# Hybrid S5 and short-convolution encoder block on eight cores: half-array products side by side, rotation products without their sum, and a finer TensorE order in the S5 stage

## The reference, cut to what matters

```python
h = rms_norm(h_stream, g_mix_pre)
u_s, x_c, b_c, c_c, gl_s, gl_c = split(h @ w_in)
# branch S: per group of 16 channels 64 complex states, forward and backward
ar, ai = exp(lr*dt)*cos(li*dt), exp(lr*dt)*sin(li*dt)
s[t] = (ar + i*ai) * s[t-1] + z * (B @ u_s[t])        # associative scan
y_s  = D*u_s + sum over both directions of  Re(C @ s)
y_s  = gelu(y_s); y_s = y_s * sigmoid(y_s @ w_glu + b_glu); y_s = y_s @ w_s_up
# branch C
y_c  = (b_c * dwconv3(c_c * x_c)) @ w_c_up
merged = sigmoid(gl_s + gb_s)*y_s + sigmoid(gl_c + gb_c)*y_c
h_stream = h_stream + rms_norm(merged @ w_o)
gate, up = split(rms_norm(h_stream) @ w_ffn_in)
h_stream = h_stream + rms_norm((silu(gate)*up) @ w_ffn_out)
```

## Time and profile before

| | |
|---|---|
| Median of 3 runs | 1840.55 us (1840.54 to 1956.79) |
| The profiled execution: time of the run | 1844.34 us |
| its span on core 1, the slowest | 1843.3 us (all cores 1825.6 to 1843.3) |
| PE busy in the span | 1766.2 us (96%), 9744 matmuls |
| DVE busy | 701.7 us (38%) |
| ACT busy | 496.3 us (27%) |
| granted clock, mean of core 1 | 0.991 |

### The profile page before, as it was taken

How to read it: one execution, slowest core, us unless ns; L and a number is a source line. 1 busy time by engine, 2 the same in 40 slices (tenths; PEclk the granted TensorE clock), 3 DMA queues, 4 the chain that set the end, 5 groups by cost and what they waited for, 6 DMA issues and landing times.

```text
span 1843.3 us, 25331 instructions; the slowest of 8 cores (1825.6 to 1843.3 us)
## 1 busy us (share of the span) xinstructions
PE 1766.2 (96%) x9744; PEld 848.0 (46%) x9744; DVE 701.7 (38%) x820; ACT 496.3 (27%) x948; POOL 118.0 (6%) x226
## 2 busy tenths in 40 slices
PE   3999999999999979889999999999999999999998
PEld 2664555544444434334444444444444444444443
DVE  4475999887786524425620110110110010101023
ACT  4554665545555420014420000000000000101010
POOL 0000000000001011100000000000000000000000
PEclk9999999999999989999999999999999999999999
DMA  9754444466667878974554446464555441443457
GB/s 236 192 152 103 79 82 83 78 114 133 123 118 160 182 143 190 220 167 138 182 121 80 69 80 112 69 112 80 100 98 94 69 79 33 77 81 66 91 126 243
DMA packets 87510, 219.06 MB, mean 119 GB/s; under 512 B 34080, under 2 KB 34592, under 8 KB 80832
## 3 DMA queue, kind: packets, MB, share of 16 engines
q0 software_dynamic: 31744, 121.71, 39.3%
q1 hardware_dynamic: 52480, 90.58, 16.4%
q10 hardware_dynamic: 3168, 5.15, 0.8%
HBM read 303.32 MB, written 35.72 MB: 184 GB/s over the span
## 4 chain that ended last, share of the span: by engine, by line
PE 82%; DMA 12%; DVE 2%; issue 2%; ACT 1%; SPq 1%; POOL 0%; ACTq 0%; DVEq 0%; POOLq 0%
PE ps L219 82%; DMA yr<-yc_d 5%; DMA wus<-w_in 2%; DMA wr<-w_in 2%; DMA xin<-xseq 1%; DMA gs_d<-tc 1%; DMA gT<-g_d 1%; PE ps L225 1%; SPq L213 1%; DMA gs_d<-ys 1%; DMA xr<-xseq 0%; DVE mgd L244 0%; DVE Pt L255 0%; POOL wus L213 0%; ACT Xt L235 0%
## 5 line engine op out<-in xcount | busy, mean ns | idle before, releaser
L219 PE MATMUL ps<-hN,wf 128*128 128x512 bf16 x2816 | 608.1, 379 | 0.0
L219 PEld LDWEIGHTS ps<-hN,wf 128*128 128x128 bf16 x2816 | 275.4, 98 | 331.8
L219 PE MATMUL ps<-hT,wr 128*128 128x512 bf16 (+1 forms) x1888 | 368.8, 351 | 5.3 <-DMA wr<-w_in 4.0
L219 PE MATMUL ps<-wfo,agr 128*128 128x512 bf16 x1408 | 304.1, 379 | 0.0
L241 DVE TENSOR_TENSOR agr<-ps,sgt 128x512 bf16<-128x512 f32 x88 | 60.9, 692 | 535.8 <-PE ps L219 535.8
L219 PEld LDWEIGHTS ps<-hT,wr 128*128 128x128 bf16 x1888 | 178.8, 97 | 175.9 <-issue 15.1
L219 PEld LDWEIGHTS ps<-wfo,agr 128*128 128x128 bf16 x1408 | 137.8, 98 | 166.1
L235 ACT ACTIVATE sgt<-ps 128x512 f32<-128x512 f32 x88 | 52.6, 598 | 535.0 <-PE ps L219 535.0
L219 PE MATMUL ps<-wo,mgd 128*128 128x512 bf16 x512 | 114.6, 386 | 5.6 <-DVE mgd L244 4.8
L241 DVE TENSOR_TENSOR facc<-ps,gp2a 128x512 f32<-128x512 f32 x24 | 16.6, 692 | 212.2 <-ACT sqj L235 151.4
L235 ACT ACTIVATE sqj<-ps 128x512 bf16<-128x512 f32 x32 | 19.1, 598 | 265.3 <-PE ps L219 265.3
(11 more groups left out here) (136 smaller groups left out, 1361.4 us busy)
## 6 DMA issues: line engine op xcount, KB each, us to landing
wf<-w_ffn_in POOLq DMA_DIRECT2D x88, 512.0 KB, 5.7
wr<-w_in POOLq DMA_DIRECT2D x51, 512.0 KB, 6.5
wfo<-w_ffn_out POOLq DMA_DIRECT2D x16, 1408.0 KB, 9.7
...
```

Source lines behind the costliest of these rows:

```text
L219: return lambda e: e.matmul(o, lhsT=l, rhs=r, start=st, stop=sp)
```

## The change

- PE: rotated-back states are no longer summed. The cosine products go to `Gt` and the sine products to a new bf16 tile `Gq`, both straight from DVE, and `out_stage` multiplies both with `M1`: 32 half products for each `(b, d)` where 16 stood (256 more in all); DVE loses one 128x1024 addition for each.
- The 16 full products `Mst` x `Ub` now stand together ahead of the half products; in `scan_stage` the four products are ordered so that neighbours go to different halves of the output.
- `prep1` makes each complex product with three real products: 10 operations of 1024 and two of 256 where 12 of 1024 stood, from two more tables (`ASUM`, `WSUM`).
- `trig`'s range reduction goes from a DVE multiply with rounding into int32 to an ACT Identity with a large bias.
- `pB` and `go` have one buffer each, no longer two. `gT` is eight tiles with keys of their own, b=0 to 4 lying on `ptmp` and `Wt` only.
- For the order: half products count half the cost, the least cost of a matmul is 0.02 and no longer 0.06 us, and D's matmul groups of 16 go in pieces of 8, between which S may come.

```diff
+    PIECE = 8
@@ mms
-        self.add("pe", fns, sum(max(0.06, it[5] / 2400.0 + 0.0025) for it in items), reads, writes, lag=lag)
+        n = self.PIECE if self.stream == "D" else len(items)
+        for i in range(0, len(items), n):
+            part = items[i:i + n]
+            self.add("pe", [one(*it[:5]) for it in part], sum(max(0.02, it[5] / 2400.0 + 0.0025) for it in part), reads, writes, lag=lag)
@@ tables
+    S.tt(ASUM, ARE[:, 0:512], AIM[:, 0:512], ALU.add, 512, [kr, ki, ("wtab", 0), ("wtab", 1)], [("tbK", 2)])
+    S.tt(WSUM, WR, WI, ALU.add, 512, [("wtab", 0), ("wtab", 1), ("tbK", 2)], [("tbK", 3)])
...
+    S.ts(sv(s_phi), sv(s_phi), 1.0 / TWO_PI, None, ALU.mult, None, 64, [sk(s_phi)], [sk(s_phi)])
@@ prep1
-        S.tt(v4(ta), cc(BR), aa(WR), ALU.mult, 1024, [pk, w0], [ka])
-        S.tt(v4(tb), cc(BI), aa(WI), ALU.mult, 1024, [pk, w1], [kb])
+        S.tt(bsum[:], re2, im2, ALU.add, 256, [pk], ["bsum"])
+        S.tt(im2, im2, re2, ALU.subtract, 256, [pk], [pk])
+        S.tt(v4(ta), cc(BR), aa(WSUM), ALU.mult, 1024, [pk, kw_s], [ka])
+        S.tt(v4(tb), cs(0), aa(WI), ALU.mult, 1024, ["bsum", w1], [kb])
         S.tt(ww(0), ta, tb, ALU.subtract, 1024, [ka, kb], [("Wt", 0)])
-        S.tt(v4(ta), cc(BI), aa(WR), ALU.mult, 1024, [pk, w0], [ka])
-        S.tt(v4(tb), cc(BR), aa(WI), ALU.mult, 1024, [pk, w1], [kb])
+        S.tt(v4(tb), cc(BI), aa(WR), ALU.mult, 1024, [pk, w0], [kb])
         S.tt(ww(1), ta, tb, ALU.add, 1024, [ka, kb], [("Wt", 1)])
@@ trig
-        S.ts(tB[:, 0:W], tA[:, 0:W], 1.0 / TWO_PI, None, ALU.mult, None, W, TK, ["trB"])
-        S.stt(tA[:, 0:W], tB[:, 0:W], -TWO_PI, tA[:, 0:W], ALU.mult, ALU.add, W, TK + ["trB"], TK)
+        S.act(tB[:, 0:W], tA[:, 0:W], AF.Identity, W, TK + [("small", 60)], ["trB"], bias=magic)
+        S.stt(tA[:, 0:W], tB[:, 0:W], MAGIC, tA[:, 0:W], ALU.subtract, ALU.subtract, W, TK + ["trB"], TK)
@@ scan_stage
-            for hh in range(2):
-                for ri in range(2):
+            for ri in range(2):
+                for hh in range(2):
...
-        S.tt(o3(1024), zs, cs, ALU.mult, 1024, PK + ["CO%d" % d], ["Qt", "Qt_hi"])
-        S.tt(o3(0), zs, ss, ALU.mult, 1024, PK + SK, ["Qt"])
-        S.tt(Gt[:, d, :, :, :].rearrange("p r a k -> p r (a k)"), Qt[:, 1024:2048].rearrange("p (r k) -> p r k", r=2), swap(Qt, 512), ALU.add, 1024,
-             ["Qt", "Qt_hi"], [("Gt", d)])
+        S.tt(Gt[:, d, :, :, :], zs, cs, ALU.mult, 1024, PK + ["CO%d" % d], [("Gt", d)])
+        S.tt(Gq[:, d, :, :, :], zs, ss, ALU.mult, 1024, PK + SK, [("Gq", d)])
@@ out_stage
+            if d == 0:
+                for gq in range(4):
+                    for dd in range(2):
+                        for hh in range(2):
+                            items.append((o(hh, gq), Mst[p][:, dd, hh, gq, :], UB[p][:, 4 * hh + gq, 2:130], gq == 0 and dd == 0, False, 128))
             for gq in range(4):
...
+                for gt, ri, gi in ((Gt, 0, 0), (Gq, 0, 1), (Gt, 1, 1), (Gq, 1, 0)):
...
-        go, gk = GO[b % 2], "go%d" % (b % 2)
+        gk = "go0"
@@ M stream
-    gT = S.tile("gT", [128, 8, 8, 128], BF16, 160384)
+    gT = [S.tile("gT%d" % b, [128, 8, 128], BF16, 162432 + 2048 * b) for b in range(8)]
...
-            S.dma(q, gT[16 * g8:16 * g8 + 16, b, :, :], src, 32768, "gT%d%s" % (b, q), reads=[("g_d", b)], writes=[("gT", b, g8)])
+            S.dma(q, gT[b][16 * g8:16 * g8 + 16, :, :], src, 32768, "gT%d%s" % (b, q), reads=[("g_d", b)], writes=[("gT%d" % b, g8)])
```

More of the change, by code:

```diff
@@ L25 @@
 SIN_S = 1.0 - 1e-5
+MAGIC = 1.5 * 2.0 ** 23
 NCORES = 8
@@ L219, in one @@
             return lambda e: e.matmul(o, lhsT=l, rhs=r, start=st, stop=sp)
-        fns = [one(*it[:5]) for it in items]
-        self.add("pe", fns, sum(max(0.06, it[5] / 2400.0 + 0.0025) for it in items), reads, writes, lag=lag)
+        n = self.PIECE if self.stream == "D" else len(items)
+        for i in range(0, len(items), n):
+            part = items[i:i + n]
+            self.add("pe", [one(*it[:5]) for it in part], sum(max(0.02, it[5] / 2400.0 + 0.0025) for it in part), reads, writes, lag=lag)
     def transposes(self, items, reads, writes, early=100000):
@@ L470, in _program @@
     S.memset(halfpi, math.pi / 2, [], [("small", 63)])
+    magic = small[:, 60:61]
+    S.memset(magic, MAGIC, [], [("small", 60)])
     LRE, LIM, LDT = lam[:, 0:64], lam[:, 64:128], lam[:, 128:192]
@@ L619, in _program @@
     Gt = S.tile("Gt", [128, 2, 2, 4, 128], BF16, 131712)
+    Gq = S.tile("Gq", [128, 2, 2, 4, 128], BF16, 141952)
     yt = S.tile("yt", [128, 8, 128], F32, 135808)
-    GO = [S.tile("go%d" % i, [128, 8, 128], BF16, 139904 + 2048 * i) for i in range(2)]
+    go = S.tile("go0", [128, 8, 128], BF16, 139904)
     def load_u(b):
@@ L659, in scan_stage @@
             items = []
-            for hh in range(2):
-                uv = UB[p][:, 4 * hh + gq, :]
-                rhs = uv[:, 0:NP] if d == 0 else mk(uv, [[-1, NP]], off=NCH - 1)
-                for ri in range(2):
-                    items.append((bs[ri][0][64 * hh:64 * hh + 64, 0:NP], Vst[p][:, d, hh, gq, 64 * ri:64 * ri + 64], rhs, True, True, NP))
+            for ri in range(2):
+                for hh in range(2):
+                    uv = UB[p][:, 4 * hh + gq, :]
+                    rhs = uv[:, 0:NP] if d == 0 else mk(uv, [[-1, NP]], off=NCH - 1)
+                    items.append((bs[ri][0][64 * hh:64 * hh + 64, 0:NP], Vst[p][:, d, hh, gq, 64 * ri:64 * ri + 64], rhs, True, True, NP // 2))
             S.mms(items, ukeys(b) + [("Vst%d" % p, d, 0), ("Vst%d" % p, d, 1)], [bs[0][1], bs[1][1]])
@@ L840, in _program @@
             q = "sp" if b < 7 else ("sp", "act", "pool")[g8 % 3]
-            S.dma(q, gT[16 * g8:16 * g8 + 16, b, :, :], src, 32768, "gT%d%s" % (b, q), reads=[("g_d", b)], writes=[("gT", b, g8)])
-    GK = [("gT", b, g8) for b in range(8) for g8 in range(8)]
+            S.dma(q, gT[b][16 * g8:16 * g8 + 16, :, :], src, 32768, "gT%d%s" % (b, q), reads=[("g_d", b)], writes=[("gT%d" % b, g8)])
+    GK = [("gT%d" % b, g8) for b in range(8) for g8 in range(8)]
     g3 = S.tile("g3", [128, 8, NTOK], BF16, 180416)
@@ L849, in _program @@
     GS = [S.tile("gs%d" % i, [128, NTOK], F32, 164032 + 4096 * i) for i in range(2)]
-    gT2 = gT[:].rearrange("p b i n -> p b (i n)")
+    gT2 = [flat(t[:]) for t in gT]
     WK = [("wgl", kq) for kq in range(4)]
     def glu(m, blk, pb, pk, ks):
-        S.mms([(pb[:], wgl[:, k, 128 * m:128 * m + 128], gT2[:, k, 512 * blk:512 * blk + 512], k == 0, k == 7, 512) for k in ks],
-              WK + [("gT", k, g8) for k in ks for g8 in range(8)], [pk])
+        S.mms([(pb[:], wgl[:, k, 128 * m:128 * m + 128], gT2[k][:, 512 * blk:512 * blk + 512], k == 0, k == 7, 512) for k in ks],
+              WK + [("gT%d" % k, g8) for k in ks for g8 in range(8)], [pk])
     first = {}
@@ L879, in _program @@
         if m in EARLY:
-            ei = EARLY.index(m) % 2
+            ei = sorted(EARLY).index(m) % 2
             gs, gk = GS[ei], ("gs%d" % ei,)
```

53 lines of the change are left out of this document (26 added, 27 removed).

## The result

The changed kernel takes 1850.2 us in the median of its runs, the kernel before 1840.9 on the same chip. The ratio is 1.0051 with a 95% interval of 1.0028 to 1.0075: some 9 us slower, where 12.4 us less were forecast. It is less than 2% and so within what was called no change, but the sign is wrong and the time lies outside the range of 1818 to 1846.

What follows compares the result with a forecast made beforehand. PE was taken to bound the kernel while S and D are mixed, DMA the merge stage. The terms summed to -12.4 us: 1844.3 to 1831.9, less 3.8 for the runs' median, 1828 us; range 1818 to 1846.

Steps and rivals of the forecast that it cites:

- More half products: PE in S5: 256 more half products at 28.8 ns each, +7.4 us, bounds 0.0 and 14 us.
- no pairs: Rival: new `Gt` and `Gq` products on PE don't run in pairs, 13.9 us instead of 7.4, 1835 us; chance 0.07.
- Changes of shape: PE's whole order: 193 changes between full and half products instead of 205, at 0.106 us each, -1.3 us.
- `Vst` products: S5's `Vst` products on PE: already run in pairs, so reordering them gains 0.
- the other bound: `Vst` products on PE: if they did not already run in pairs, one pass less would gain 5.2 us.
- DVE and ACT: S5's elementwise work: some 35 us less on DVE, an Identity more per direction on ACT, covered by PE's work: 0.
- One buffer for `pB` and `go`: S5 blocks: the load and store take 7.8 us within a block of some 50 us, so covered: 0.
- `gT` loads earlier: D's last 40 us: fewer `gT` loads on SP free the `gs_d` stores; PE's `Xt` wait -3.2 us, slow clock -1.2 us.
- The boundary: D's end to GLU's other 86 matmuls: 9.1 us instead of 21.0, -11.9 us; those matmuls at full clock, -2.2 us.
- the boundary stays: Rival at D's end: last `gs_d` stores leave SP late again, `gT` lands 21 us behind D's end, 1844 us; chance 0.20.
- The merge stage: 697 to 798 us, bound by DMA: moves earlier as a whole, 0, bounds -5 and +5 us.
- The rival of the early burst: Early `gT` loads on SP hold the convolution's `yc_d` stores, DVE and PE wait, 5 to 15 us, 1838 us; chance 0.10.

Runs made afterwards that it cites:

- e8: Kernel before with only tables by three products in `prep1` and the range reduction on ACT; PE's products, groups and costs as before: ratio 1.0043.
- e9: Kernel before with one edit, D's matmul groups of 16 in pieces of 8: ratio 1.0054.
- e7: Changed kernel with D's matmul groups whole again (16, not 8), all else as changed: ratio 1.0014.

## Why the prediction was wrong, step by step

1. *More half products, +7.4 us*: right. 32 of the new ones, with the change of shape ahead of them, take 0.99 us, 596.90 to 597.89, or 31 ns each; the steps between pairs are 0.11 us for four. The rival "no pairs" (54 ns each) falls. The row on which it rests and the next, with 16 full products in 0.99 us before them:

```profile
595.91 1.06 PE L221 MATMUL ps<-Ub,Mst 128*128 128x128 bf16 x16
596.90 0.23 PE L221 MATMUL ps<-Gt,M 64*128 64x128 bf16 x2
...
597.89 0.30 PE L221 MATMUL ps<-Ub,Vst 128*64 128x130 bf16 x4
```

2. *Changes of shape, -1.3 us*: the count was of the order and stands; the block is 1.98 us for 48 products where the earlier trace rows has 2.18 for 32, which bears out both the drain (in the Trainium skill's TensorEngine Tiling (Array Packing) it stands under Key Properties, not in the Overview) and the price of 0.106 us.

3. *`Vst` products, 0*: right. Four of 258 columns take 0.34 us in the new order (582.80 to 583.14), 0.35 in the old. The 5.2 us of the other bound, which the Trainium skill (TensorEngine Tiling (Array Packing), Key Properties) would let one expect from more neighbours in different halves, are not there: this case's rows show the same time in either order.

```profile
582.80 0.41 PE L221 MATMUL ps<-Ub,Vst 128*64 128x258 bf16 x4
583.14 8.81 PE L221 MATMUL ps<-hT,wr 128*128 128x512 bf16 x39
```

4. *DVE and ACT, 0*: wrong. The work is covered, as it said, but the order isn't independent of it: e8 has this step, but for the sums, and costs 8 us.

5. *One buffer for `pB` and `go`, 0*: its own condition ("DVE would wait, and D's operations behind it, only if it landed some 10 us late") did not come about where PE was held; no wait of PE leads to either. But DVE now waits five times for `pB`, 11.9 us in all and 3.3 at most, and in the kernel before not once; a block takes 60 us, not 50. Not tried alone.

6. *`gT` loads earlier, -3.2 and -1.2 us*: wrong. The `gs_d` stores still took 10 us and ACT still stood 8.25 us; two small queues of loads (5 and 3 of b=6) stood among them, and the stores' own travel, not only their place in the queue, was long. `Xt` cost 5.0 us and not 0 (9.3 in the mean of eight cores).

7. *The boundary, -11.9 and -2.2 us*: right to half a us (9.6 for 9.1), and so the rival "the boundary stays" falls. In part that is luck: the b=7 loads were issued 13.7 us behind the start of the last S5 group and not 9.4, and landed 4.1 us after and not 6.5. The last was there at 679.66 us, as the 42 matmuls ended. The 84 matmuls recorded of the second part take 18.72 us at full clock.

8. *The merge stage, 0*: right. From the up-projection's start to the end the changed kernel takes as long as before (+5.6 and +5.3).

**The step that failed** is in none of the eight by name. The prediction priced PE's new order by its changes of shape alone ("but D's pieces of 8 let S in at more places", -1.3 us) and held D's groups to be movable for nothing because PE is full. PE was full in the earlier trace rows since its order had been made so that loads and stores landed in time; a new order has to earn that again. It missed 12.7 us of new gaps and the slow clock behind them: the pieces alone moved D's end by 23.2 us (e9), and the changed kernel without them has it back within 2.3 us (e7). The rival of the early burst was the nearest: it named the place (540 to 580 us), the mechanism (`ys`, `yc_d`) and 5 to 15 us, and was given 0.10 and only in company with the full gain of the rest. Its part came true there (5.8 us), but the larger one, `wr` and `Xt` through the pieces, was no rival at all. In the range each unknown cost was bounded by rows except that of the order itself.
